# Rotary halves swapped by VectorE out of PSUM, routing cut to what the first expert needs, and the last experts' pieces in another order

## Chip, cores and metric

One core of one Trainium2 chip runs the whole program as one launch. The metric is device time in microseconds (us) of that core, the median of the runs.

## What is computed

Two blocks follow each other on 512 tokens of width 1024, in float32. The first (two layers of latent attention with a convolution, cross attention and SwiGLU) is not touched. The second is:

```python
def apply_rotary(t, cos, sin):                 # q and k of attention (24 heads) and of retention (8 heads)
    t1, t2 = jnp.split(t.astype(jnp.float32), 2, axis=-1)        # halves of 32 channels
    return jnp.concatenate([t1 * c - t2 * s, t1 * s + t2 * c], axis=-1)

def hierarchical_moe(x2, ...):                 # 8 groups of 8 experts, 2 experts of one group per token
    group_p = softmax(x2 @ w_group + b_group);  g_w, g_idx = top_k(group_p, 1)
    sel_logits = (x2 @ w_expert + b_expert) of the chosen group
    e_w, e_idx = top_k(softmax(sel_logits), 2); e_w = e_w / sum(e_w)
    gate = g_w * e_w;  eid = g_idx * 8 + e_idx
    ... # each token's row goes to its two experts: (silu(xb @ w1[e]) * (xb @ w3[e])) @ w2[e]
    ... # y[token] = sum of gate * its two rows
```

Between them stand dilated window attention, retention in both directions and a gated merge. After the experts comes a residual sum and an RMS norm.

## The kernel before

**Lanes and marks.** Five programs (TensorE, ScalarE, VectorE, GpSimd as POOL, SyncE) are written in order by hand. Every instruction may tick a semaphore and note a mark (`e.tick("both")`), and others wait for the mark (`e.wait_ge(*at("both"))`). PSUM's eight banks go round in one queue: `banks.take` takes the bank given back longest ago and waits for the mark that `banks.give` named.

**Weight pieces.** `pieces` lists all weights as pieces of up to 1 MB (`self.plan`) in the order of use. SyncE issues one load after the other, each into the slot of `self.slots` with the same number. TensorE appends a slot again when it has used a piece (`release`), so piece n waits until the slot's last piece was used. Until the merge there are three slots; a piece is split there into a high and a low part (ScalarE copies the high part, VectorE subtracts, lines 558 and 566) and a product takes three matmuls per 128 channels. The experts' weights are not split: six pieces per expert (w1, w3 and w2, two each), in thirteen slots: the three, two early ones, five late ones, two in `xT` and one in `norm_room`.

**Attention.** Four pairs of heads. A pair has 14 items (`pair_items`): six products of q and k, [128 channels, 512 tokens] each, and eight of v. The first pair's items run back to back; those of the next pair are laid two by two into the 8 steps of a pair. A step is: scores `near` and `far`, an item, transposes of the probabilities of two steps before, an item, the output of three steps before. A q or k item is rotated in this way: ScalarE copies the bank to `raws`, TensorE multiplies `swap_a` (a permutation with signs) with it (`rotate_pe`), VectorE multiplies the swapped bank with the sine table, POOL the raw copy with the cosine table, and VectorE adds them (`rotate_dve`, `rotate_pool`). The swap of item n - 1 stands behind the product of item n.

**Retention.** After the gate (four pieces) come four products for q and four for k (`retention_pe`, line 1982), each followed directly by its swap. VectorE and ScalarE also make the decay tables there.

**Router.** `router_pe` (line 2307) transposes the normalised tokens of tiles 2 and 3 and multiplies four tiles with the router's weights. `router_dve` (line 2400) chooses the group and two experts by one-hot rows, exponentiates through ScalarE, makes the gates, `picks` (one-hot rows of 64 experts for each choice) and `both`. TensorE counts with triangular and all-one matrices (14 products of 64 columns: rank of every token in its expert, and the totals). Then VectorE makes `local` (rank in the expert or -1), the table of further blocks (used only where an expert has over 64 tokens), and the slots of both choices for the final combine.

**Experts.** `experts_pe` (line 2566) runs n = 0 to 65. For even n it gathers the rows of experts n and n + 1 by multiplying the one-hot matrix `chosen` with the tokens, and turns them; for n from 1 on: the products w1 and w3 of expert n - 1, then the w2 product of expert n - 2, then the transposes of expert n - 1's hidden rows. `chosen` is made by VectorE from `local` (`experts_dve`, line 2652). ScalarE applies silu, copies and stores. In the combine, POOL fetches each token's two rows from DRAM and VectorE adds them up.

Of the kernel before, what the change touches and what calls it, by code (L numbers as in the profile page):

```python
# [16 lines left out]
P = 128  # L17
# [37 lines left out]
NEG = -1.0e30  # L55
VCOLS = NG * P // 2
# [134 lines left out]
class Net:  # L191
# [69 lines left out]
    def memory(self):  # L261
# [7 lines left out]
        self.swap_a = self.sb("swap_a", [P, P])  # L269
# [158 lines left out]
        self.local = carve("local", NT, EXPERTS)  # L428
# [34 lines left out]
    def pieces(self):  # L463
# [53 lines left out]
        for half in range(2):  # L517
            by_rows("mixer out", a["w_out_2"][0], 0, KD, half * BANK, (half + 1) * BANK)
        for ex in range(EXPERTS):
            for name in ("moe_w1_2", "moe_w3_2", "moe_w2_2"):  # L520
# [283 lines left out]
    def setup_act(self, e):  # L804
# [9 lines left out]
        for name, dst, src in (("pos", self.pos_i, a["positions"][0].partition_broadcast(P)),  # L814
                               ("freq", self.freq, a["c_freq"]), ("cols", self.cols[:, :], a["cols"]),
                               ("swap_q", self.swap_q[:, :], a["c_swap_q"]), ("mask_q", self.mask_q, a["c_mask_q"]),
                               ("swap_a", self.swap_a[:, :], a["c_swap_a"])):
            e.dma_start(dst, src).then_inc(*e.lands("setup_loads", "setup_landed", name))
# [19 lines left out]
    def angles_dve(self, e):  # L838
# [7 lines left out]
        e.wait_ge(*self.at("setup_landed", "swap_a"))  # L846
# [890 lines left out]
    def rotate_pe(self, e, pair, n):  # L1737
        bank = self.banks.take(e, "a_swap", pair, n)
        e.wait_ge(*self.at("a_raw", pair, n))
        e.matmul(bank[:, :], self.swap_a[:, :], self.raws[(pair * 2 * NG + n) % 2], start=True, stop=True).then_inc(  # L1740
            *e.tick("pe", "a_swap", pair, n))
        self.banks.give(("a_swap", pair, n), "a_sin", pair, n)
# [10 lines left out]
    def rotate_pool(self, e, pair, n):  # L1753
        raw = self.raws[(pair * 2 * NG + n) % 2]
        e.wait_ge(*self.at("pe", "a_swap", pair, n))
# [4 lines left out]
    def item_pe(self, e, pair, item):  # L1760
        kind, n = item
        if kind == "qk":
# [11 lines left out]
            if n:  # L1774
                self.rotate_pe(e, pair, n - 1)
# [11 lines left out]
        if n == 0:  # L1787
            self.rotate_pe(e, pair, 2 * NG - 1)
# [193 lines left out]
    def retention_pe(self, e):  # L1982
# [3 lines left out]
        for label in ("retention q", "retention k"):  # L1986
            for c4 in range(4):
# [6 lines left out]
                if c4 % 2:  # L1994
                    self.release(e, n)
                banks.give((label, c4), "r_raw", label, c4)
                bank = banks.take(e, "r_swap", label, c4)
                e.wait_ge(*at("r_raw", label, c4))
                e.matmul(bank[:, :], self.swap_a[:, :], self.raw_r[c4 % 2], start=True, stop=True).then_inc(
                    *e.tick("pe", "r_swap", label, c4))  # L2000
                banks.give(("r_swap", label, c4), "r_sin", label, c4)
# [101 lines left out]
    def retention_dve(self, e):  # L2103
# [38 lines left out]
        for label, buf in (("retention q", self.q_r), ("retention k", self.k_r)):  # L2142
            for c4 in range(4):
                if c4 % 2 == 0:
                    self.dve_piece(e, label)
                e.wait_ge(*at("pe", "r_swap", label, c4))
                e.tensor_tensor(buf[:, c4, :], self.bank("r_swap", label, c4)[:, :], self.sin_r, ALU.mult).then_inc(
                    *e.tick("r_sin", label, c4))
# [43 lines left out]
    def retention_pool(self, e):  # L2192
# [9 lines left out]
        for label in ("retention q", "retention k"):  # L2202
            for c4 in range(4):
                raw = self.raw_r[c4 % 2]
                e.wait_ge(*self.at("pe", "r_swap", label, c4))
# [101 lines left out]
    def router_pe(self, e):  # L2307
# [7 lines left out]
        for i in range(NT):  # L2315
            if i < 2:
                self.rows_to_T_pe_f32(e, i + 2)
# [685 lines left out]
```

## Time and profile before

| | |
|---|---|
| median of 3 runs | 3482.52 us (3480.45 to 3487.75) |
| the profiled execution | 3485.61 us, its span 3483.7 us |
| TensorE busy | 3244.1 us, 93% |
| VectorE busy | 1316.7 us, 38% |
| ScalarE busy | 876.0 us, 25% |
| POOL busy | 131.3 us, 4% |
| mean granted clock of TensorE | 0.961 |
| attention | about 1596 to 1960 us |
| retention | about 1960 to 2198 us |
| merge | 2198 to 2403 us |
| router up to the first gather | 2403 to 2453 us |
| experts | 2453 to 3444 us, DMA at 425 to 426 GB/s from 2530 on |
| combine | 3444 to 3484 us |

PE is TensorE's matmuls, PEld its weight loads, DVE VectorE, ACT ScalarE. A name ending in q (SPq) is an engine's queue at which DMAs are issued. An f32 product is recorded as two matmul instructions. "[2.54 <-DMA piece]" behind a row is the idle time of the engine before it and what ended it. L120 and the like are lines of small wrappers, so rows are told apart by the names of their tiles.

### The profile page before, as it was taken

The numbers are of one execution on the slowest core, as the hardware profiler recorded it, in microseconds if no ns is written. First come the engines' busy times: TensorE is split into PE (matmuls) and PEld (weight loads), VectorE is DVE, ScalarE is ACT, GpSimd is POOL, SyncE is SP. The second block draws the span as 40 slices with busy tenths as digits, with TensorE's granted clock in tenths as the row PEclk, the third lists the DMA queues.
The fourth block names the chain that finished last, engine by engine and source line by source line (L and its number), as shares of the span: only waits on it lengthen the run. The fifth ranks groups of instructions, "written<-read, shape, count | busy, mean of one in ns | idle before, by whom it ended". The sixth has DMA issues, their size and how long they took to land.

```text
span 3483.7 us, 35772 instructions
## 1 busy us (share of the span) xinstructions
PE 3244.1 (93%) x15128; PEld 2240.5 (64%) x15128; DVE 1316.7 (38%) x2223; ACT 876.0 (25%) x1387; POOL 131.3 (4%) x122
## 2 busy tenths in 40 slices
PE   9999999999999999998999989998799999999994
PEld 7677788887677788886888766677333433334341
DVE  5765633345765633334334436434211111111112
ACT  3452322222442222222333421222111111111111
POOL 0000000000000000001001010001000000000001
PEclk9999999999999999999999999998899999999997
DMA  4122123223122122232213220225699999999996
GB/s 170 59 85 85 61 91 103 94 100 112 60 85 85 61 91 97 97 109 80 67 45 98 66 73 31 67 97 192 250 426 426 426 425 426 426 425 426 426 425 239
DMA packets 229541, 627.62 MB, mean 180 GB/s; under 512 B 14784, under 2 KB 136512, under 8 KB 179968
## 3 DMA queue, kind: packets, MB, share of 16 engines
q1 hardware_dynamic: 207888, 581.47, 43.1%
q10 hardware_dynamic: 19296, 35.68, 2.9%
q0 software_dynamic: 2192, 8.13, 0.8%
q8 instruction: 121, 1.98, 0.2%
q14 instruction: 44, 0.36, 0.0%
HBM read 600.32 MB, written 22.81 MB: 179 GB/s over the span
## 4 chain that ended last, share of the span: by engine, by line
PE 67%; DMA 17%; DVE 10%; ACT 2%; POOL 2%; issue 1%; ACTq 0%; SPq 0%; DVEq 0%; POOLq 0%
PE bank L120 65%; DMA piece<-in_moe_w 4%; DMA piece_high<-in_moe_w 3%; DMA mT_slot<-in_moe_w 3%; DMA xT<-in_moe_w 3%; DVE gate_acc L138 2%; PE bank L123 2%; DVE x_tok L138 1%; POOL root L135 1%; DMA memT<-in_moe_w 1%; DMA norm_room<-in_moe_w 1%; DMA y_att_slot<-in_moe_w 1%; DVE stat L153 1%; DVE piece_rounded L135 1%; ACT piece_high_rounded L126 1%
## 5 line engine op out<-in xcount | busy, mean ns | idle before, releaser
L120 PE MATMUL bank<-xT_rounded,piece_high_rounded 128*128 128x512 f32 (+1 forms) x1408 | 550.5, 391 | 6.2 <-DVE xT_low_rounded L135 6.2
L135 DVE TENSOR_TENSOR piece_rounded<-piece,piece_high_rounded 128x2048 fp32r<-128x2048 f32 (+1 forms) x156 | 342.4, 2198 | 558.9 <-ACT piece_high_rounded L126 558.7
L120 PE MATMUL bank<-xT_rounded,piece_rounded 128*128 128x512 f32 (+1 forms) x1408 | 538.3, 382 | 0.0
L120 PE MATMUL bank<-xT_low_rounded,piece_high_rounded 128*128 128x512 f32 (+1 forms) x1408 | 534.3, 379 | 0.0
L135 DVE TENSOR_TENSOR gate_and_hidden<-gate_and_hidden,bank 64x512 f32<-64x512 f32 x64 | 69.2, 1081 | 836.9 <-ACT gate_and_hidden L126 836.9
L126 ACT ACTIVATE piece_high_rounded<-piece 128x2048 fp32r<-128x2048 f32 (+1 forms) x156 | 283.4, 1820 | 261.7 <-DMA piece<-in_ffn_w_down 102.3
L120 PEld LDWEIGHTS bank<-xT_rounded,piece_high_rounded 128*128 128x128 f32 x1408 | 266.2, 189 | 61.9 <-DVE xT_low_rounded L135 7.4
L120 PEld LDWEIGHTS bank<-xT_low_rounded,piece_high_rounded 128*128 128x128 f32 x1408 | 265.8, 189 | 55.9 <-issue 4.4
L120 PEld LDWEIGHTS bank<-xT_rounded,piece_rounded 128*128 128x128 f32 x1408 | 264.4, 188 | 56.4
L120 PE MATMUL bank<-piece,xeT 128*64 128x512 f32 x488 | 239.4, 645 | 18.7 <-DMA norm_room<-in_moe_w 6.1
L120 PE MATMUL bank<-piece_high,xeT 128*64 128x512 f32 x464 | 185.3, 630 | 12.3 <-DMA piece<-in_moe_w 9.0
L120 PE MATMUL bank<-xT,xeT 128*64 128x512 f32 x312 | 161.3, 666 | 14.7 <-DMA piece_high<-in_moe_w 9.1
L126 ACT ACTIVATE gate_and_hidden<-bank 64x512 f32<-64x512 f32 x64 | 37.9, 592 | 499.7 <-PE bank L120 499.7
L138 DVE SCALAR_TENSOR_TENSOR gate_acc<-hT,cols,gate_acc 128x512 f32<-128x512 f32 x240 | 163.2, 743 | 0.0
L120 PE MATMUL bank<-mT_slot,xeT 128*64 128x512 f32 x304 | 151.7, 655 | 11.7 <-DMA piece_high<-in_moe_w 11.7
L120 PE MATMUL bank<-piece_high_rounded,xT_rounded 128*128 128x192 f32 (+1 forms) x448 | 150.3, 336 | 4.4 <-DVE xT_low_rounded L135 2.7
L120 PE MATMUL bank<-piece_high_rounded,xT_low_rounded 128*128 128x192 f32 (+1 forms) x448 | 147.2, 329 | 0.0
L120 PE MATMUL bank<-piece_rounded,xT_rounded 128*128 128x192 f32 (+1 forms) x448 | 146.7, 327 | 0.0
L120 PE MATMUL bank<-piece_high_rounded,hidT_rounded 128*128 128x512 f32 x352 | 138.1, 392 | 0.0
L120 PE MATMUL bank<-piece_rounded,hidT_rounded 128*128 128x512 f32 x352 | 137.5, 391 | 0.0
L120 PE MATMUL bank<-piece_high_rounded,hidT_low_rounded 128*128 128x512 f32 x352 | 137.5, 391 | 0.0
L120 PEld LDWEIGHTS bank<-piece,xeT 128*64 128x64 f32 x488 | 69.4, 147 | 88.5 <-issue 88.5
(337 smaller groups left out, 5050.8 us busy)
## 6 DMA issues: line engine op xcount, KB each, us to landing
piece<-in_moe_w SPq DMA_DIRECT2D x90, 1024.0 KB, 16.5
piece_high<-in_moe_w SPq DMA_DIRECT2D x88, 1024.0 KB, 16.5
xT<-in_moe_w SPq DMA_DIRECT2D x59, 1024.0 KB, 16.6
mT_slot<-in_moe_w SPq DMA_DIRECT2D x58, 1024.0 KB, 17.1
piece<-in_ffn_w_in SPq DMA_DIRECT2D x40, 1024.0 KB, 5.1
memT<-in_moe_w SPq DMA_DIRECT2D x30, 1024.0 KB, 15.8
y_att_slot<-in_moe_w SPq DMA_DIRECT2D x30, 1024.0 KB, 16.7
norm_room<-in_moe_w SPq DMA_DIRECT2D x29, 1024.0 KB, 16.9
```

The costliest lines, as they stand in the source:

```text
L120: return self.engine.matmul(*a, **k) if self.engine is not None else Nothing()
L123: return self.engine.transpose(*a, **k) if self.engine is not None else Nothing()
L126: return self.engine.activation(*a, **k) if self.engine is not None else Nothing()
L135: return self.engine.tensor_tensor(*a, **k) if self.engine is not None else Nothing()
L138: return self.engine.scalar_tensor_tensor(*a, **k) if self.engine is not None else Nothing()
L153: return self.engine.bn_stats(*a, **k) if self.engine is not None else Nothing()
```

## The change

1. Swaps. `swap_a`, its load, `rotate_pe` and the swap products of retention go. VectorE multiplies each group of 32 lanes of the product's own bank with the sine table and writes it to the neighbouring group of lanes; the signs are in the table. The bank is given back only after that (before: after ScalarE's copy). POOL's cosine product waits for ScalarE's copy. For k of retention the scale is applied in the four operations.
2. Router. Tile 3's transposes move behind tile 1's products. Products by one-hot rows of the four tiles are joined into single operations; `both` is made from the sum of the one-hot rows; rank is four wide products and the totals get a bank and products of their own. `local` is FAR * both - rank in one operation, compared with FAR - iota. The counts and the table of further blocks (`counts_dve`), slots (`slots_dve`) and gates (`gates_dve`, `gates_act`) move into the first turns of the experts' loops.
3. Last experts. The plan's last pieces are w1, w3 of expert 62, w1, w3 of 63, then w2 of both; at n = 64 the transposes of expert 63's hidden rows stand before the w2 product of expert 62.

```diff
+        for ex in range(EXPERTS):
+            for name in ("moe_w1_2", "moe_w3_2"):
+                for part in range(2):
+                    self.up_pieces.setdefault(ex, []).append(len(plan))
+                    plan.append((name, self.together(a[name][0, ex], part), False))
+            for ready in () if ex == EXPERTS - 2 else (ex,) if ex < EXPERTS - 2 else (ex - 1, ex):
+                for part in range(2):
+                    self.down_pieces.setdefault(ready, []).append(len(plan))
+                    plan.append(("moe_w2_2", self.together(a["moe_w2_2"][0, ready], part), False))
...
-    def rotate_pe(self, e, pair, n):
-        bank = self.banks.take(e, "a_swap", pair, n)
-        e.matmul(bank[:, :], self.swap_a[:, :], self.raws[(pair * 2 * NG + n) % 2], start=True, stop=True).then_inc(
+    def swapped(self, b):
+        other = b + 1 - b % 2 * 2
+        return slice(b * 32, (b + 1) * 32), slice(other * 32, (other + 1) * 32)
...
     def rotate_dve(self, e, pair, n):
-        e.wait_ge(*self.at("pe", "a_swap", pair, n))
-        e.tensor_tensor(buf, self.bank("a_swap", pair, n)[:, :], self.sin_a, ALU.mult).then_inc(*e.tick("a_sin", pair, n))
+        e.wait_ge(*self.at("pe", "a_qk", pair, n))
+        e.wait_ge(*self.at("a_raw", pair, n))
+        for b in range(4):
+            to, other = self.swapped(b)
+            e.tensor_tensor(buf[to, :], bank[other, :], self.sin_a[other, :], ALU.mult).then_inc(
+                *(e.tick("a_sin", pair, n) if b == 3 else e.tick()))
...
-            self.banks.give(("a_qk", pair, n), "a_raw", pair, n)
+            self.banks.give(("a_qk", pair, n), "a_sin", pair, n)
...
-                e.matmul(bank[:, :], self.swap_a[:, :], self.raw_r[c4 % 2], start=True, stop=True).then_inc(
+                for b in range(4):
+                    to, other = self.swapped(b)
+                    e.scalar_tensor_tensor(out=buf[to, c4, :], in0=self.bank(label, c4)[other, :],
+                                           scalar=RQK ** -0.5 if label == "retention k" else 1.0,
+                                           in1=self.sin_r[other, :], op0=ALU.mult, op1=ALU.mult).then_inc(
...
-            if i < 2:
-                self.rows_to_T_pe_f32(e, i + 2)
+            if i % 2 == 0:
+                self.rows_to_T_pe_f32(e, 2 + i // 2)
...
-        for i in range(NT + 1):
-            last = min(i, NT - 1)
-            for j in range(last + 1):
-                ins = e.matmul(bank[:, i * EXPERTS:(i + 1) * EXPERTS], self.tri if j == i else self.ones,
+        e.matmul(bank[:, 0:NT * EXPERTS], self.tri, both, start=True, stop=False).then_inc(*e.tick())
+        for n in range(1, NT):
+            ins = e.matmul(bank[:, n * EXPERTS:NT * EXPERTS], self.ones, both[:, 0:(NT - n) * EXPERTS], start=False,
+                           stop=(n == NT - 1))
+        bank = banks.take(e, "count")
+        for j in range(NT):
+            ins = e.matmul(bank[:, 0:EXPERTS], self.ones, self.both[:, j, :], start=(j == 0),
...
+        e.tensor_tensor(self.t8, ohs[0], ohs[1], ALU.add).then_inc(*e.tick())
+        e.tensor_tensor(self.both.rearrange("p i (g e) -> p i g e", g=GROUPS),
+                        oh_g.unsqueeze(3).broadcast_to([P, NT, GROUPS, PER_GROUP]),
+                        self.t8.unsqueeze(2).broadcast_to([P, NT, GROUPS, PER_GROUP]), ALU.mult).then_inc(*e.tick("both"))
+        e.wait_ge(*at("pe", "rank"))
+        e.scalar_tensor_tensor(out=self.local.rearrange("p i e -> p (i e)"), in0=self.both.rearrange("p i e -> p (i e)"),
+                               scalar=FAR, in1=self.bank("rank")[:, 0:NT * EXPERTS], op0=ALU.mult,
+                               op1=ALU.subtract).then_inc(*e.tick("local"))
...
     def experts_pe(self, e):
+            if n == EXPERTS:
+                self.hidden_T_pe(e, n - 1)
             if n < EXPERTS and n % 2 == 0:
                 self.rows_T_pe(e, n // 2)
...
-            if 1 <= n <= EXPERTS:
+            if 1 <= n < EXPERTS:
                 self.hidden_T_pe(e, n - 1)
...
     def experts_act(self, e):
+            if n == 1:
+                self.gates_act(e)
...
     def experts_dve(self, e):
             if n < EXPERTS and n % 2 == 0:
                 self.rows_T_dve(e, n // 2)
+            if n == 0:
+                self.counts_dve(e)
+            if n in (1, 2):
+                self.slots_dve(e, n - 1)
+            if n == 3:
+                self.gates_dve(e)
```

## Rows read from the trace of the kernel before

**Rows 1.** The page, part 4: the chain of waits by engine, shares of the span.
```profile
PE 67%; DMA 17%; DVE 10%; ACT 2%; POOL 2%; issue 1%; ACTq 0%; SPq 0%; DVEq 0%; POOLq 0%
```
**Rows 2.** Windows: start:end, length, busy us per engine, granted clock, DMA share, GB/s.
```profile
2440.00:2450.00 10.00, 0.00 (x0) 0.00 (x0) 9.11 (x27) 0.00 (x0) 0.00 (x0) 0.50 0.00 0
...
2510.00:2520.00 10.00, 9.29 (x48) 3.68 (x48) 2.37 (x3) 1.03 (x3) 0.00 (x0) 1.00 1.02 429
```
**Rows 3.** Timeline of TensorE, first pair: start, duration, engine, line, tiles.
```profile
1615.22 1.02 PE L120 MATMUL bank<-raws,swap_a 128*128 128x512 f32 x2
...
1621.58 1.02 PE L120 MATMUL bank<-raws,swap_a 128*128 128x512 f32 x2
```
**Rows 4.** The chain in order of time, attention and retention: start, duration, what.
```profile
1750.12 15.85 PE bank L120 x70
1766.62 15.85 PE bank L120 x70
...
1970.34 33.88 PE bank L120 x144
...
2023.32 6.64 PE bank L120 x26
2030.63 6.64 PE bank L120 x26
...
2070.24 55.40 PE bank L120 x244
```
**Rows 5.** Groups of VectorE by form: count, busy us, mean ns, idle before.
```profile
L135 DVE TENSOR_TENSOR piece_rounded<-piece,piece_high_rounded 128x2048 fp32r<-128x2048 f32 x39 | 89.0, 2289 | 138.7 <-ACT piece_high_rounded L126 138.7
...
L135 DVE TENSOR_TENSOR gate_and_hidden<-gate_and_hidden,bank 64x512 f32<-64x512 f32 x64 | 69.2, 1081 | 836.9 <-ACT gate_and_hidden L126 836.9
...
L135 DVE TENSOR_TENSOR heads_q<-turn_raw,turn_sin 32x512 f32<-32x512 f32 x16 | 10.9, 684 | 3.0 <-POOL turn_raw L135 2.6
```
**Rows 6.** Timeline of VectorE in retention.
```profile
2133.74 2.47 DVE L135 TENSOR_TENSOR weigh<-bank,memT 128x512 f32<-128x512 f32 x4
```
**Rows 7.** Timeline of VectorE in the router.
```profile
2420.86 0.46 DVE L135 TENSOR_TENSOR logits<-bank,router_b 128x288 f32<-128x288 f32 x1 [12.21 <-PE bank L120]
...
2422.47 0.19 DVE L135 TENSOR_TENSOR g<-logits,v 128x32 f32<-128x32 f32 x1
...
2430.82 0.42 DVE L135 TENSOR_TENSOR both<-picks,picks 128x256 f32<-128x256 f32 x1
2437.57 0.42 DVE L129 COPY rank<-bank 128x256 f32<-128x256 f32 x1 [6.33 <-PE bank L120]
...
2438.82 0.23 DVE L132 TENSOR_SCALAR extra<-bank 128x64 f32<-128x64 f32 x1
...
2444.19 0.42 DVE L135 TENSOR_TENSOR wide<-picks,rank 128x256 f32<-128x256 f32 x1
...
2451.93 0.89 DVE L135 TENSOR_TENSOR chosen_rounded<-iota,local 128x128 fp32r<-128x128 f32 x4
```
**Rows 8.** Timeline of TensorE, router's products and first gather.
```profile
2408.71 1.97 PE L123 MATMUL bank<-ident,hn_low 128*128 128x128 f32 x8 [2.25 <-DVE hn_low L138]
2410.47 10.36 PE L120 MATMUL bank<-router_w,xT 128*128 128x72 f32 x48
...
2452.87 0.79 PE L120 MATMUL bank<-hn_high_rounded,chosen_rounded 128*128 128x512 f32 x1 [15.34 <-DVE chosen_rounded L135]
```
**Rows 9.** Timeline of SyncE's DMA queue: first issue after each release.
```profile
2467.66 0.33 SPq L162 DMA_DIRECT2D piece<-in_moe_w  x1
...
2482.66 0.33 SPq L162 DMA_DIRECT2D mT_slot<-in_moe_w  x1
```
**Rows 10.** Timeline of TensorE, last expert.
```profile
3425.83 1.09 PE L120 MATMUL bank<-piece,xeT 128*64 128x512 f32 x1 [2.54 <-DMA piece<-in_moe_w]
...
3434.25 1.90 PE L120 MATMUL bank<-memT,ehidT 128*64 128x512 f32 x8
...
3440.32 1.94 PE L120 MATMUL bank<-piece_high,ehidT 128*64 128x512 f32 x8 [2.07 <-ACT ehidT L126]
```

More of the change, by code:

```diff
@@ L2447, in router_dve @@
-        for n in range(2):
-            for i in range(NT):
-                out = picks[n][:, i, :].rearrange("p (g e) -> p g e", g=GROUPS)
-                e.wait_ge(*e.own())
-                e.tensor_tensor(out, oh_g[:, i, :].unsqueeze(2).broadcast_to([P, GROUPS, PER_GROUP]),
-                                ohs[n][:, i, :].unsqueeze(1).broadcast_to([P, GROUPS, PER_GROUP]), ALU.mult).then_inc(
-                    *e.tick())
-        e.wait_ge(*e.own())
-        e.tensor_tensor(self.both, picks[0], picks[1], ALU.add).then_inc(*e.tick("both"))
@@ L2457, in router_dve @@
-        bank = self.bank("rank")
-        rank, local = self.rank, self.local
-        e.wait_ge(*at("pe", "rank"))
-        e.tensor_copy(rank.rearrange("p i e -> p (i e)"), bank[:, 0:NT * EXPERTS]).then_inc(*e.tick())
-        count = bank[:, NT * EXPERTS:(NT + 1) * EXPERTS]
-        e.wait_ge(*e.own())
-        e.scalar_tensor_tensor(out=local, in0=rank, scalar=1.0, in1=self.both, op0=ALU.add, op1=ALU.mult).then_inc(*e.tick())
-        e.wait_ge(*e.own())
-        e.tensor_scalar(local, local, -1.0, None, ALU.add).then_inc(*e.tick("local"))
@@ new lines, in counts_dve @@
+    def counts_dve(self, e):
+        at = self.at
+        rank, ends, extra = self.rank, self.ends, self.extra
+        gmax, m1, m2, d_ = self.v4[0], self.v4[3], self.v4[4], self.v4[5]
+        e.tensor_tensor(self.g8, self.logits[:, :, 0:GROUPS], gmax.unsqueeze(2).broadcast_to([P, NT, 8]),
+                        ALU.subtract).then_inc(*e.tick("g8"))
+        e.tensor_tensor(d_, m2, m1, ALU.subtract).then_inc(*e.tick("apart"))
+        e.tensor_copy(rank.rearrange("p i e -> p (i e)"), self.bank("rank")[:, 0:NT * EXPERTS]).then_inc(
+            *e.tick("rank_copied"))
+        count = self.bank("count")[:, 0:EXPERTS]
+        e.wait_ge(*at("pe", "count"))
@@ L2487, in router_dve, with gates_dve @@
         e.tensor_copy(self.more_i, self.more_f).then_inc(*e.tick("more"))
[L2488 to L2493 removed]
+    def gates_dve(self, e):
+        at = self.at
+        gsum, d_, r_ = self.v4[1], self.v4[5], self.v4[6]
+        e.wait_ge(*at("g8_exp"))
+        e.tensor_reduce(gsum, self.g8, AX.X, ALU.add).then_inc(*e.tick())
+        e.wait_ge(*e.own())
+        e.reciprocal(gsum, gsum).then_inc(*e.tick())
+        e.wait_ge(*at("apart_exp"))
+        e.tensor_scalar(r_, d_, 1.0, None, ALU.add).then_inc(*e.tick())
+        e.wait_ge(*e.own())
+        e.reciprocal(r_, r_).then_inc(*e.tick())
+        e.wait_ge(*e.own())
+        e.tensor_tensor(self.moe_gates[0], gsum, r_, ALU.mult).then_inc(*e.tick())
+        e.wait_ge(*e.own())
+        e.tensor_tensor(self.moe_gates[1], self.moe_gates[0], d_, ALU.mult).then_inc(*e.tick())
@@ new lines, in slots_dve @@
+    def slots_dve(self, e, n):
+        rk, ex, bg, fl = self.v4[7:11]
+        pick, wide = self.picks[n], self.wide
+        e.wait_ge(*e.own())
+        e.tensor_tensor(pick.rearrange("p i (g e) -> p i g e", g=GROUPS),
+                        self.oh_g.unsqueeze(3).broadcast_to([P, NT, GROUPS, PER_GROUP]),
+                        self.ohs[n].unsqueeze(2).broadcast_to([P, NT, GROUPS, PER_GROUP]), ALU.mult).then_inc(*e.tick())
+        for out, by in ((rk, self.rank), (ex, self.row(self.iota64, EXPERTS)), (bg, self.row(self.begins, EXPERTS))):
@@ L2511, in gather_pe @@
+        e.scalar_tensor_tensor(out=self.slot_f[n], in0=bg, scalar=float(CAP), in1=rk, op0=ALU.mult,
+                               op1=ALU.add).then_inc(*e.tick())
+        e.wait_ge(*e.own())
+        e.tensor_copy(self.slot_i[n], self.slot_f[n]).then_inc(*e.tick("slots", n))
     def gather_pe(self, e, q):
```

147 lines of the change are left out of this document (59 added, 88 removed).

## The prediction

> **What bounds the kernel now.** I read the chain of waits first. By engine it is 67% TensorE, 17% DMA and 10% VectorE [rows 1], so a microsecond taken off TensorE counts wherever the chain runs on it. Then the windows. In 2440:2450 TensorE does nothing, VectorE is 91% busy and the DMA moves 0 GB/s; in 2510:2520 it moves 429 GB/s at a share of 1.02 [rows 2]. From about 2483 to 3425 the kernel is one saturated stream of expert weights (384 pieces of 1 MB, one in 2.46 us at 427 GB/s). The stream has 13 slots; they fill before the first expert is computed, and then the DMA stands until TensorE gives slots back. TensorE's granted clock in 2440:2450 is 0.50, the lower of its two levels (1.2 GHz), with TensorE idle [rows 2]; "half clock" below means that. So the end follows the moment at which the stream runs for good. Three places can move it: attention and retention (TensorE-bound, ahead of it), the routing (ahead of the first released slots), and what comes after the last piece.
>
> **Attention's swaps, 24 products.** A rotation now costs one f32 product of 512 columns. Swap follows swap after 6.36 us in the first pair [rows 3]; between them lie 24 products at 0.229 us, 5.50 us. So a swap takes 0.86 us of TensorE. Nothing hid it: TensorE has no gap there, and a step with two such items starts 16.50 us after the one before [rows 4]. Removed: 24 x 0.86 = 20.6 us.
>
> What is added lies on VectorE: one 128x512 multiplication becomes four of 32x512. The trace of before has no 32-lane operation that reads PSUM in another group of lanes than it writes, four in a row. Nearest rows: a 32x512 product whose inputs and output lie in different groups of 32 lanes took 684 ns; the dearest 512-element product, with strided operands and one in PSUM, 1081 ns [rows 5]; four 128x512 products out of PSUM back to back took 2.47 us together, 0.62 each [rows 6]. Bounds of one: 0.62 and 1.08 us. I take 0.72, the first row plus the 0.03 us seen between waiting neighbours, since it has the same lanes and size. Four make 2.9 us in place of 0.69, so 2.2 us more per rotation.
>
> Is there room? A heavy step (two rotations) shrinks to 16.50 - 1.72 = 14.8 us. VectorE does in it: softmax 2.1, one split of a weight piece 2.3 [rows 5], two rotations of 2.9 + 0.7, together 11.6 us. The rotation of the first item follows the split, which waits for ScalarE's half of it; laid out in order, VectorE is done some 0.8 us before the next scores are. Even late scores don't stop TensorE, which transposes them two steps later. The bank of a product is now held until VectorE has read it, about 11 us into the next step; banks go round seven at a time and six are taken per step, so it is wanted 4 us after that. In the first pair an item costs VectorE 2.9 + 0.7 + 1.15 (half a split) = 4.8 us against TensorE's 5.5. The cover holds; cost zero. Without it each 0.1 us of a multiplication would cost 0.8 us in each of 9 heavy steps.
>
> A rule of the Trainium skill speaks against the four: VectorE: DVE Perf Modes, section "Two Vector instructions with no wait between them", says that an instruction whose inputs or output start in another quadrant than those of the one before is held until everything earlier has finished. By it the four don't overlap, 4 x 0.72; without it they would run like rows 6, 2.5 us. No row shows four such in a row; the sum moves by about 1 us, in retention.
>
> **Retention's swaps, 8 products.** Here TensorE also waits each time for ScalarE's copy. A period is 7.31 us, of which 5.50 is the product [rows 4]. The whole, from the gate's end at 2004.2 to the end of the last swap at 2071.1, takes 66.9 us, the wait behind the decay tables included (chain rows at 1970.34 and 2070.24). After: 8 x 5.50 = 44.0, if splits come in time. VectorE needs per item 2.9 + 0.7 + 1.15, and 2.4 once for tables: 40 us for eight, so it follows closely; laid out in order, the split of the second piece of k comes about 1.8 us late (behind the rotations of q and the table that ScalarE needs first). I take 46 us. Gain 21 us; bounds 14 (0.86 + 0.85 each and no more, 8 times) and 23.
>
> **Routing, up to the first gather.** Before, the last router product ends at 2420.83 and the gather starts at 2452.87 [rows 8].
> - The fourth tile's transposes now come after the second tile's products, so the 2.25 us idle before 2408.71 is filled by 16 products [rows 8]. If these run at the full clock they vanish there: 16 x 0.216 = 3.4 us gained. At half clock from the start 2.2; if filling the gap keeps the clock up for all, 7. I take 3.4.
> - The vector chain up to both took 10.38 us (2420.86 to 2431.24 [rows 7]). Counted anew: logits 0.49; three choices of the best, 15 small operations of 0.22; two small ones more; the masked logits, their sum and the final product at 0.45 each: 5.6 us. Gain 4.8.
> - Rank: 28 instructions, 6.3 us, to 2437.57 [rows 7]. Now products of 256, 192, 128 and 64 columns. At half clock a 512-column product costs 1.72 (twice the 0.86), a short one not under 0.43: 0.86 + 0.64 + 0.43 + 0.43 = 2.4 us. Gain 3.9.
> - From rank to gather 15.3 us [rows 7, 8]: two copies, counts, the further blocks' table, both slot chains. Now one operation out of PSUM (0.45) and the comparison (0.93), beside 8 count instructions on TensorE, 1.75 us, which stand in front of the gather: 1.8 us. Gain 13.5.
> Together 25.6 us: the gather starts near 2427.3 by the old clock. POOL's low halves (done 2421.6) and the first pieces (landed by then) don't hold it.
>
> What was moved comes back. The counts (6.2 us) run after the xeT copies while TensorE is in expert 0's 7.1 us product: they end 1.6 us ahead of need. The slots of choice 0 (0.45 + 3.9 us from 2444.19, [rows 7]) now stand before the comparison for experts 2 and 3; TensorE's next gather and expert 1's product are queued behind it: 4.4 us later, and 0.5 us more for a longer time at half clock. The rest (second slots, gates, ScalarE's two exponentials and two table loads) falls into gaps of 8 to 13 us. The first four slots were released at 2467.66, the next four at 2482.66 [rows 9]; four pieces are 9.8 us, so the DMA stood again before 2482.66. It runs for good from that second release, which moves by 25.6 - 4.9 = 20.7 us. Bounds 9 and 25.
>
> **The tail.** Expert 63's first weights now come two pieces earlier in the stream, 4.9 us. Its product started at 3425.83 after 2.54 us of waiting for the DMA, ran 3 us at half clock and ended at 3434.25 [rows 10]. Now it starts at 3423.4, in an unbroken run, and needs 6.9 to 7.0 us: 3430.4. Then silu, product and transposes (2.4 us), and both outputs, 3.6 us each: 3440.0 in place of 3443.98 (from 3440.32 plus 3.66). Gain 4.0 us, bounds 1 and 5. The two last down pieces land by 3430.3. The combine behind it doesn't change.
>
> Sum: 20.6 + 21 + 20.7 + 4.0 = 66.3 us. The profiled execution took 3485.6 us (span 3483.7 and 1.9 around it): 3419.3 by its own time. The median of the runs lies 3.1 us lower, which gives 3416 us.
>
> **Rivals.**
> - Postponed routing costs its full length. All 16.4 us of counts, slots and gates delay the first slots; for it: they stand in VectorE's queue before work that TensorE needs. Against: VectorE idles 8 us (2460.4 to 2468.3) there. Then the routing yields 25.6 - 16.4 = 9 us, the time is 3428. Chance 0.15.
> - VectorE becomes the bound of rotations. At 1.08 us per multiplication the heavy step still fits (14.5 of 14.8); the first pair's items take 6.2 instead of 5.5, retention's 6.5 instead of 5.75: 10 us lost, 3426. For it: 1081 ns in rows 5. Against: those operands are strided. Chance 0.1.
> - The clock stays up over the router's products and rank, and the second gather is hardly late: 6 to 9 us more, 3408. Chance 0.12.
> - Slower: shifted reads out of PSUM go lane group by lane group and cost D. A heavy step is then 5.8 + 8D, a first item 1.85 + 4D, a retention item 2.15 + 4D, against 16.5, 6.36 and 8.4 before. With 24.7 us gained elsewhere the sum is zero at D = 1.54 us; at 2.2 us it is 128 x 0.66 = 84 us slower, 3567. Only the 684 ns row, not out of PSUM, speaks against it. Chance 0.03.
> - The change doesn't do what it says, for example since banks held longer stop TensorE as much as the swaps did: 3455 to 3480. Chance 0.02.
>
> **How the numbers follow.** My forecast has 0.58: 3416, own range 3409 to 3424. With the first three rivals and the bounds of the terms the range for 8 in 10 is 3402 to 3434. A measurement of this kernel tells about 0.2%, 7 us. Faster 0.96, within 0.01, slower 0.03.
>
> **What would show it.** No swap products; TensorE still without gaps in 1600 to 1900 and heavy steps near 14.8 us; 32x512 products near 0.69 us; retention's q and k in about 46 us; the first gather 10 us after the last router product instead of 32; the first two releases of slots about 19.9 us apart instead of 15.0; experts' DMA share unchanged; last product's end to combine unchanged. It is wrong if TensorE waits for VectorE in attention, if the second release comes over 25 us after the first, or if the stream has gaps later.

## The result, and the profile after

The changed kernel takes 3441.97 us (median of 4 runs, 3437.72 to 3446.06), the kernel before 3484.17 us beside it: a ratio of 0.9879, 95% interval 0.9861 to 0.9897. It is 42 us faster. 3416 us was forecast, with a range of 3402 to 3434 us; the time lies 8 us above that range.

The profiled execution has a span of 3444.2 us instead of 3483.7. Page, part 1 (busy us by engine) and part 4 (the chain by engine, which answers to [rows 1]):

```profile
PE 3215.6 (93%) x15052; PEld 2226.0 (65%) x15052; DVE 1387.9 (40%) x2311; ACT 876.3 (25%) x1388; POOL 136.7 (4%) x122
...
PE 65%; DMA 17%; DVE 12%; ACT 3%; POOL 2%; issue 1%; ACTq 0%; SPq 0%; DVEq 0%; POOLq 0%
```

VectorE's share of the chain grew from 10 to 12%: some of its work stands on the path now. By stages, cut at the same instructions in both traces (us saved, of 39.5):

| stage | before | after | saved | forecast |
|---|---|---|---|---|
| start to first attention product | 1596.40 | 1598.96 | -2.6 | 0 |
| attention | 373.9 | 375.0 | -1.0 | 20.6 |
| retention's q, k and v (end of the gate's products to the last v product) | 111.7 | 93.6 | 18.1 | 21 |
| retention's gate, rest of retention, merge | 321.6 | 320.8 | 0.8 | 0 |
| third tile's transposes to first released slots | 64.0 | 40.5 | 23.5 | 25.6 |
| first to second release | 15.0 | 20.5 | -5.5 | -4.9 |
| second release to the end | 1001.0 | 994.9 | 6.1 | 4.0 |

Attention is where the forecast failed. Its heavy steps (two q/k items) are as forecast, 14.8 us from softmax to softmax in the second and third pair. The first light steps (two v items) behind them are not. VectorE's timeline, second pair (start, duration, engine, line, operation, tiles; each `aprobs<-bank,masks` is one step's softmax):

```profile
1787.21 0.69 DVE L142 CUSTOM_DVE_ANT_0 aprobs<-bank,masks 128x512 f32<-128x512 f32 x1 [1.81 <-PE bank L121]
...
1791.11 1.76 DVE L136 TENSOR_TENSOR piece_rounded<-piece,piece_high_rounded 128x1536 fp32r<-128x1536 f32 x1 [1.75 <-ACT piece_high_rounded L127]
1792.90 2.84 DVE L136 TENSOR_TENSOR ks<-bank,sin_a 32x512 f32<-32x512 f32 x4
1795.84 0.69 DVE L136 TENSOR_TENSOR ks<-ks,raws 128x512 f32<-128x512 f32 x1
1801.14 0.69 DVE L142 CUSTOM_DVE_ANT_0 aprobs<-bank,masks 128x512 f32<-128x512 f32 x1 [4.61 <-PE bank L121]
```

The next softmaxes come at 1801.14, 1812.82 and 1821.95: steps of 13.93 and 11.68 us, then 9.13. Before, the same two took 10.00 and 9.12. TensorE's timeline at that place, its waits in attention (us in total, times, longest), and the windows (columns as in [rows 2]):

```profile
1793.08 0.28 PE L121 MATMUL bank<-piece_high_rounded,xT_low_rounded 128*128 128x192 f32 x1
1795.79 0.43 PE L121 MATMUL bank<-aprobsT,vs 128*64 128x128 f32 x2 [2.44 <-DVE ks L136]
```
```profile
PE bank L121 <- DVE ks L136: 6.9, 3, 2.4
```
```profile
1786.00:1798.00 12.00, 9.56 (x72) 8.73 (x70) 7.24 (x13) 4.02 (x8) 0.52 (x1) 0.93 0.22 79
1798.00:1806.00 8.00, 8.00 (x31) 6.55 (x30) 2.04 (x7) 1.03 (x2) 0.00 (x0) 0.50 0.01 2
1806.00:1840.00 34.00, 34.00 (x242) 29.51 (x242) 11.29 (x30) 12.85 (x24) 0.00 (x0) 0.99 0.19 63
```

Read together: the last q/k product's bank comes free when VectorE has multiplied out of it. VectorE first splits the piece of v, and that split waits until 1791.11 for ScalarE's half. Only then come the four multiplications, whose last ends at 1795.74. TensorE wanted the bank at 1793.35 and stands for 2.44 us. Behind the wait its granted clock is 0.50 (1.2 GHz) for the whole window from 1798 to 1806, with TensorE busy throughout. Such a wait comes once in three of the four pairs: 2.0 us in the first, 2.44 us in each of the next two.

The router. TensorE's products now stand between the transposes (the third tile's begin at 2388.32), all at the full clock:

```profile
2389.20 3.69 PE L121 MATMUL bank<-router_w,xT 128*128 128x72 f32 x32
2393.37 1.09 PE L124 MATMUL bank<-ident,hn_low 128*128 128x128 f32 x8 [0.48 <-DVE hn_low L139]
2394.29 3.69 PE L121 MATMUL bank<-router_w,xT 128*128 128x72 f32 x32
```

The last ends 9.7 us after the third tile's transposes begin. Before, these began at 2403.68 and the last product ended 17.2 us later, at 2420.83 [rows 8]. VectorE's chain behind it, and GpSimd beside it:

```profile
2398.74 2.14 DVE L136 TENSOR_TENSOR t<-logits,v 128x32 f32<-128x32 f32 x1
2400.91 2.26 DVE L136 TENSOR_TENSOR t<-t,down 128x32 f32<-128x32 f32 x1
2403.21 0.19 DVE L148 TENSOR_REDUCE v<-t 128x4 f32<-128x32 f32 x1
2403.43 2.04 DVE L136 TENSOR_TENSOR oh_g<-down,v 128x32 f32<-128x32 f32 x1
...
2407.05 0.19 DVE L136 TENSOR_TENSOR t<-t,down 128x32 f32<-128x32 f32 x1
...
2409.29 0.42 DVE L136 TENSOR_TENSOR both<-oh_g,t 128x256 f32<-128x256 f32 x1
```
```profile
2396.16 9.26 POOL L136 TENSOR_TENSOR hn_low_rounded<-hn_low,hn_high_rounded 128x1024 fp32r<-128x1024 f32 x4 [4.96 <-ACT hn_high_rounded L127]
```

The chain was counted at 5.6 us and takes 11.7 (from 2398.02). One and the same 128x32 operation takes 2.26 us while GpSimd works and 0.19 us after it has stopped; three such operations are stretched.

The releases (SyncE's queue, answering to [rows 9]), and what holds the second, on TensorE and VectorE:

```profile
2428.78 0.33 SPq L163 DMA_DIRECT2D piece<-in_moe_w  x1
...
2449.30 0.33 SPq L163 DMA_DIRECT2D mT_slot<-in_moe_w  x1
```
```profile
2430.49 0.42 DVE L136 TENSOR_TENSOR picks<-oh_g,ohs 128x256 f32<-128x256 f32 x1
...
2434.75 0.89 DVE L136 TENSOR_TENSOR chosen_rounded<-from_far,local 128x128 fp32r<-128x128 f32 x4
```
```profile
2435.70 0.80 PE L121 MATMUL bank<-hn_high_rounded,chosen_rounded 128*128 128x512 f32 x1 [4.73 <-DVE chosen_rounded L136]
```

The slots of choice 0 run from 2430.49 to 2434.84 and the comparison for experts 2 and 3 stands behind them, as forecast. The last two experts, by the chain in order of time, answer to [rows 10]:

```profile
3389.54 7.04 PE bank L121 x32
...
3398.78 7.04 PE bank L121 x32
```

### The profile page after: what moved, and what is told of

Its sections match the earlier page's. It is cut to its first block, busy times and chain, and to the rows that moved or that the text cites. A ratio compares the mean times of both kernels' runs of the same rounds, so it can differ in the third digit from the quotient of the medians.

```text
span 3444.2 us, 35709 instructions
## 1 busy us (share of the span) xinstructions
PE 3215.6 (93%) x15052; PEld 2226.0 (65%) x15052; DVE 1387.9 (40%) x2311; ACT 876.3 (25%) x1388; POOL 136.7 (4%) x122
## 4 chain that ended last, share of the span: by engine, by line
PE 65%; DMA 17%; DVE 12%; ACT 3%; POOL 2%; issue 1%; ACTq 0%; SPq 0%; DVEq 0%; POOLq 0%
PE bank L121 63%; DMA piece_high<-in_moe_w 4%; DMA mT_slot<-in_moe_w 3%; DMA piece<-in_moe_w 3%; DMA xT<-in_moe_w 3%; DVE gate_acc L139 2%; PE bank L124 2%; DVE x_tok L139 2%; POOL root L136 1%; DMA memT<-in_moe_w 1%; DVE piece_rounded L136 1%; DMA norm_room<-in_moe_w 1%; DMA y_att_slot<-in_moe_w 1%; ACT piece_high_rounded L127 1%; DVE stat L154 1%
## 5 line engine op out<-in xcount | busy, mean ns | idle before, releaser
L121 PE MATMUL bank<-piece_high,xeT 128*64 128x512 f32 x464 | 187.1, 642 | 15.4 <-DMA piece<-in_moe_w 9.3
```

Source lines behind the costliest of these rows:

```text
L121: return self.engine.matmul(*a, **k) if self.engine is not None else Nothing()
```

## Experiments

All are the changed kernel with one edit. "Release" is the first DMA issue after the first or second set of slots came free, counted from the third tile's transposes.

**1. The sine products ahead of the split.**

```diff
     # item_dve, v items
-        if n % NT == 0:
-            self.dve_piece(e, "attention v")
         if n == 0:
             self.rotate_dve(e, pair, 2 * NG - 1)
+        if n % NT == 0:
+            self.dve_piece(e, "attention v")
```

> The changed kernel, with VectorE making the sine products of the last q/k item ahead of its split of the v piece, so that the bank of the last q/k product comes free about 1.8 us earlier. Theory A (attention's gain went into a bank that TensorE waits for, and into the half clock that follows): the 2.4 us wait of the 12 attention products on bank and aprobsT in pairs 2 and 3 goes to under 0.8 us, the granted clock stays at 1.00 in the 10 us behind it, the two steps of 13.9 and 11.7 us of each pair come to 9.2 to 10 us each, and the kernel takes 15 to 20 us less than the changed one (3422 to 3427 us). Rival A2 (VectorE's added work is what binds attention, whatever its order): the steps lengthen as before, the wait only moves, and the time stays within 2 us of the changed kernel's 3442 us. Rival A3 (the wait goes but the v piece's split is late by 2.8 us and TensorE waits for that instead): the wait of the v product of 2 to 3 us takes its place, gain 0 to 5 us.

Measured: 3423.39 us, ratio 0.9828 (0.9812 to 0.9845), 18.6 us below the changed kernel. VectorE:

```profile
1778.74 2.84 DVE L136 TENSOR_TENSOR ks<-bank,sin_a 32x512 f32<-32x512 f32 x4
1781.69 0.69 DVE L136 TENSOR_TENSOR ks<-ks,raws 128x512 f32<-128x512 f32 x1
1782.30 1.75 DVE L136 TENSOR_TENSOR piece_rounded<-piece,piece_high_rounded 128x1536 fp32r<-128x1536 f32 x1
1785.70 0.69 DVE L142 CUSTOM_DVE_ANT_0 aprobs<-bank,masks 128x512 f32<-128x512 f32 x1 [1.65 <-PE bank L121]
```

TensorE's waits in attention have no entry for `ks` any more. From softmax to softmax, the light steps behind the heavy ones of the second and third pair are 9.12 or 9.13 us and the heavy ones 14.8; attention takes 353.8 us, 20.1 less than before the change, where 20.6 was forecast. The same instructions fit, so VectorE's added work doesn't bind attention (A2 falls). TensorE's one wait for a split there is 1.2 us, against 1.0 in the changed kernel, so the split is not late (A3 falls).

**2. Attention's products back.** Retention, routing and tail stay as changed.

```diff
+        bank = self.banks.take(e, "a_swap", pair, n)
+        e.wait_ge(*self.at("a_raw", pair, n))
+        e.matmul(bank[:, :], self.swap_a[:, :], self.raws[(pair * 2 * NG + n) % 2], start=True, stop=True).then_inc(
+            *e.tick("pe", "a_swap", pair, n))
...
-        for b in range(4):
-            to, other = self.swapped(b)
-            e.tensor_tensor(buf[to, :], bank[other, :], self.sin_a[other, :], ALU.mult).then_inc(
+        e.tensor_tensor(buf, self.bank("a_swap", pair, n)[:, :], self.sin_a, ALU.mult).then_inc(*e.tick("a_sin", pair, n))
```

> The changed kernel, with attention's halves swapped by TensorE's 24 products as in the kernel before, and the rest (retention, routing, order of the last pieces) as changed. Theory A: attention's part of the change gave only 1.1 us in the profiled execution, so this one takes 0 to 3 us more than the changed kernel (3442 to 3445 us), with heavy steps of 16.5 us, no step of 13.9 us and no half clock in them. Rival (the swaps' removal is worth its 20.6 us, and what is lost was lost elsewhere, as in the first 1600 us): 15 to 20 us more, about 3460 us.

Measured: 3441.06 us, 0.9881 (0.9864 to 0.9897), the same as the changed kernel. Attention takes 374.7 us, with steps of 16.5, 10.0 and 9.12. So the measured gain of 42 us came from the other three parts, within the 8 us or so that the two ratios leave open.

**3. The wait doubled.**

```diff
+        for b in range(4 if n == 2 * NG - 1 else 0):
+            to, other = self.swapped(b)
+            e.tensor_tensor(buf[to, :], bank[other, :], self.sin_a[other, :], ALU.mult).then_inc(*e.tick())
+        if n == 2 * NG - 1:
+            e.wait_ge(*e.own())
```

> The changed kernel, with VectorE's four sine multiplications of the last q/k item of each pair made twice (the second time with the same values), so that the bank of that product comes free about 2.9 us later. Theory A (the bank wait, and the clock behind it, are what attention lost): TensorE's three longest waits grow from 2.4 to about 5.3 us, so pairs 2, 3 and 4 lose 2.9 us each or more, 8.7 to 14 us in all, and the kernel takes 3450 to 3458 us. Rival (the wait shown is only where the time is booked, and VectorE had room there): the waits and the time stay within 2 us of the changed kernel's.

Measured: 3454.35 us, 0.9922 (0.9906 to 0.9939), 13.5 us above the changed kernel run beside it (4). TensorE's waits:

```profile
PE bank L121 <- DVE ks L136: 15.5, 3, 5.3
```

```profile
1802.00:1815.00 13.00, 12.24 (x54) 10.65 (x55) 3.42 (x9) 1.97 (x5) 0.00 (x0) 0.54 0.00 1
```

The waits grow by 2.9 us each, by what is added to VectorE in front of the bank, 8.6 us in all; the step with the wait goes from 13.9 to 17.2 us. The window lies behind the second pair's wait. Attention takes 385.9 us, 10.9 more than in the first trace, where the half clock also stood behind all three waits, and 22.8 more than in the trace of (4), where it stood behind one only. So the waits account for 8.6 us; that the rest is a longer time at half clock fits the windows, but no run separates it.

**4. The changed kernel again.**

> The changed kernel once more, without an edit. Four profiles with its attention code have had attention lengths of 375.0, 369.8, 372.4 and 366.4 us, and the start of attention between 1594.2 and 1599.2 us, though no instruction there differed. If the half clock behind the bank wait is a matter of how long TensorE is held at it, and not of the instructions, this run lies among them: attention 366 to 376 us, start 1594 to 1600 us, median 3436 to 3446 us. Rival (the differences came from the edits after all): 375.0 us and 1599.0 us within 0.5 us.

Measured: 3440.9 us, runs from 3427.65 to 3442.87, 0.9885 (0.9868 to 0.9901). The profiled one has a span of 3425.9 us, attention of 363.1 us (below the 366 expected) and a start at 1593.64 us. The waits are the same, the clock behind them is not; the second pair's wait lies in this window:

```profile
PE bank L121 <- DVE ks L136: 6.9, 3, 2.4
```
```profile
1782.00:1790.00 8.00, 5.56 (x42) 4.61 (x41) 5.42 (x9) 0.61 (x3) 0.00 (x0) 1.00 0.01 2
```

Here the clock stays at 1.00 and the steps are 11.64 and 9.12 us: the bare wait costs 2.5 us. With the half clock behind it, as in the trace after, it costs 7.4 (13.93 + 11.68 against 2 x 9.12). Seven profiles with this same attention code and this wait gave 375.0, 363.1, 372.4, 369.8, 366.4, 375.9 and 373.4 us, the two without the wait 353.8 and 353.9. The -2.6 us ahead of attention belongs to such scatter too: the start lies between 1593.6 and 1599.6 us in the twelve profiles, and the changed kernel alone had it at 1593.6 and at 1599.0.

**5. The low halves on VectorE.** They are made while it waits for the router's products.

```diff
     # router_dve, behind from_far; removed from router_pool
+        for i in range(NT):
+            e.wait_ge(*at("hn_high", i))
+            e.wait_ge(*at("pe", "hnT", i, 4))
+            self.low_of(e, self.hn_low[:, i, :], self.hn_low[:, i, :], self.hn_high[:, i, :]).then_inc(*e.tick("hn_split", i))
     # router_act: each high half straight behind its tile, not all four at the end
+                self.high_of(e, self.hn_high[:, i - 1, :], self.hn_low[:, i - 1, :]).then_inc(*e.tick("hn_high", i - 1))
```

> The changed kernel, with the low halves of the four normalised tiles made by VectorE before it waits for the router products, in place of GpSimd, and ScalarE's high halves one at a time behind its evictions. Theory B (VectorE's operations with two inputs in SBUF are held up while GpSimd's tensor_tensor runs): the three small 128x32 operations take 0.2 us each again in place of 2.1, the chain from the last router product to the last condition takes 5.6 to 6.2 us in place of 11.7, and the kernel takes 4 to 6 us less (3436 to 3438 us). Rival B2 (the small operations are slow for what they read, whatever GpSimd does): they stay near 2.1 us and the time stays or grows by what VectorE's four low halves take (about 4 us). Rival B3 (the chain is short but the four low halves start too late on VectorE and push it back): chain 5.6 us, start 3 to 5 us later, gain 0 to 2 us.

Measured: 3434.20 us, 0.9862 (0.9845 to 0.9879). VectorE:

```profile
2386.90 4.61 DVE L136 TENSOR_TENSOR hn_low_rounded<-hn_low,hn_high_rounded 128x1024 fp32r<-128x1024 f32 x4
2391.58 0.46 DVE L136 TENSOR_TENSOR logits<-bank,router_b 128x288 f32<-128x288 f32 x1
...
2392.30 0.19 DVE L136 TENSOR_TENSOR t<-logits,v 128x32 f32<-128x32 f32 x1
...
2396.98 0.43 DVE L136 TENSOR_TENSOR both<-oh_g,t 128x256 f32<-128x256 f32 x1
```

The chain takes 5.8 us, and the comparison comes 5.9 us earlier. The first release moves from 40.5 us (38.8 in six others of these profiles, where the gather itself ran at the full clock) to 35.4, though the gather ran at a clock of 0.51 here. The four halves fit into the gap (1.15 us each instead of GpSimd's 2.3), so B3 falls. The total alone would not show it: the ratios differ by 0.0017, and their two half-widths together are 0.0025.

**6. GpSimd made to wait.** Nothing is added on VectorE.

```diff
     # router_pool, ahead of the low halves
+        e.wait_ge(*self.at("both"))
```

> The changed kernel with one wait more on GpSimd: it begins the low halves of the four tiles only when VectorE's chain of conditions has ended. No instruction is added on VectorE. Theory B (it is GpSimd's simultaneous tensor_tensor that stretches VectorE's small operations): the three 128x32 operations of 2.0 to 2.3 us take 0.19 us, the chain from the last router product to the last condition takes 5.6 to 6 us in place of 11.7; GpSimd's 9.3 us then lie behind it, where the rank, the local and the chosen operations meet them, so that the gather starts 0 to 6 us earlier than in the changed kernel or up to 4 us later: 3437 to 3446 us. Rival B2 (the operations are slow because of where they read): they stay at 2.0 to 2.3 us.

Measured: 3438.16 us, 0.9863 (0.9848 to 0.9879), runs from 3430.9 to 3448.98. GpSimd, then VectorE:

```profile
2404.66 9.35 POOL L136 TENSOR_TENSOR hn_low_rounded<-hn_low,hn_high_rounded 128x1024 fp32r<-128x1024 f32 x4 [12.73 <-DVE both L136]
```
```profile
2399.46 0.19 DVE L136 TENSOR_TENSOR t<-logits,v 128x32 f32<-128x32 f32 x1
...
2404.15 0.43 DVE L136 TENSOR_TENSOR both<-oh_g,t 128x256 f32<-128x256 f32 x1
...
2407.28 0.42 DVE L139 SCALAR_TENSOR_TENSOR local<-both,bank 128x256 f32<-128x256 f32 x1 [2.70 <-PE bank L121]
2407.73 6.62 DVE L136 TENSOR_TENSOR chosen_rounded<-from_far,local 128x128 fp32r<-128x128 f32 x4
```

The chain takes 5.8 us again, and now the comparison is stretched, 6.62 us for four instead of 0.90. The stretch goes with GpSimd's time and hits whatever VectorE does in it with two inputs in SBUF. `local`, with one input in SBUF and one in PSUM, takes its 0.42 us in the middle of it. B2 falls. The first release stays at 40.2 us: moving the place where the two engines meet gains nothing.

**7. Slots and gates behind the comparisons.**

```diff
     # experts_dve
-            if n in (1, 2):
-                self.slots_dve(e, n - 1)
-            if n == 3:
+            if n in (2, 4):
+                self.slots_dve(e, n // 2 - 1)
+            if n == 6:
```

> The changed kernel, with VectorE's two slot steps and its gates put behind the chosen pieces (n 2, 4 and 6 instead of 1, 2 and 3). Theory C (the second release is late because the first slots stand ahead of the second chosen piece on VectorE): the first two SP releases stand 15 to 16.5 us apart instead of 20.5, TensorE's 4.7 us wait for the rounded second chosen piece goes to about 0.5 us, and the kernel takes 4 to 5 us less (3437 to 3438 us). Rival (a transfer that the slots feed, or the piece's own landing, ends the second stretch): the wait at TensorE goes but the releases stay 19 to 20.5 us apart, and the time stays at 3442 us.

Measured: 3432.11 us (3423.54 to 3439.56), 0.9848 (0.9823 to 0.9873). The releases:

```profile
2421.49 0.33 SPq L163 DMA_DIRECT2D piece<-in_moe_w  x1
...
2436.74 0.33 SPq L163 DMA_DIRECT2D mT_slot<-in_moe_w  x1
```

They are 15.25 us apart, not 20.5 (19.4 to 19.6 in six others of these profiles): the delay was the slots, as forecast, and it is worth 4 to 5 us. The median fell further than that, by 10 us, but its runs are 16 us apart, and attention, not edited, took 5.2 us less in this profile than in the first.

**8. Retention's products back.**

```diff
-                banks.give((label, c4), "r_sin", label, c4)
+                banks.give((label, c4), "r_raw", label, c4)
+                bank = banks.take(e, "r_swap", label, c4)
+                e.wait_ge(*at("r_raw", label, c4))
+                e.matmul(bank[:, :], self.swap_a[:, :], self.raw_r[c4 % 2], start=True, stop=True).then_inc(
+                    *e.tick("pe", "r_swap", label, c4))
+                banks.give(("r_swap", label, c4), "r_sin", label, c4)
```

> The changed kernel with retention's halves swapped by 8 products of TensorE as in the kernel before. The stretch from the end of the retention gate to the end of the v products was 121.4 us before and 103.3 us after: it goes back to about 121 us, and the kernel takes 17 to 19 us more (3459 to 3461 us). Rival (part of the 18 us came with other states of the buffers left by attention, not from the products): 112 to 118 us in the stretch and 9 to 15 us more.

Measured: 3452.14 us, 0.9915 (0.9900 to 0.9930), only 10 us above the changed kernel (the ratios differ by 0.0036, their two half-widths together are 0.0023: 4 to 21 us). In the trace the stretch, cut as in the table, grows from 93.6 to 109.0 us, by 15.4; on the expectation's scale that is 118.7, between the two theories. The windows over it, before and in this run:

```profile
2004.00:2116.00 112.00, 102.16 (x401) 76.86 (x399) 36.35 (x36) 28.11 (x28) 10.31 (x8) 0.95 0.21 71
```
```profile
2001.00:2112.00 111.00, 101.15 (x405) 76.08 (x405) 36.47 (x37) 28.73 (x29) 10.79 (x8) 0.98 0.21 72
```

The same instructions and the same eight waits, with a mean clock of 0.98 in place of 0.95. A mean of 0.95 is a tenth of the stretch at half clock, 11 us, in which 5.6 are lost; 0.98 loses 2.2. That difference of 3.4 covers the missing 2.7. The changed kernel's stretch also had a mean clock of 0.98 (2007.6 to 2101.3), so at the same clock the products cost 15.4 us, and the other 2.7 of the table's 18.1 are the clock's doing. The rival's cause, buffers left in another state by attention, doesn't show: the waits are the same.

**9. The tail undone.**

```diff
-            for ready in () if ex == EXPERTS - 2 else (ex,) if ex < EXPERTS - 2 else (ex - 1, ex):
+            for ready in (ex,):
...
-            if n == EXPERTS:
-                self.hidden_T_pe(e, n - 1)
```

> The changed kernel with the order of the last experts' pieces and transposes as before. What the tail is worth: the time behind the second release goes from 994.9 us back to about 1001 us, and the kernel takes 4 to 6 us more (3446 to 3448 us). Rival: the 6.1 us that the profile shows behind the second release come from the earlier start of the pieces and not from the tail's order; then it stays within 2 us of 3442 us.

Measured: 3441.52 us (3432.29 to 3449.38), 0.9880 (0.9859 to 0.9900): no difference that the times can show. The trace shows it: second release to the end 1001.2 us, as before the change, against 993.7 to 997.5 in the ten profiles with the new tail. The tail is worth 3.7 to 7.5 us. Attention, not edited, took 366.4 us in this profile, 8.6 less than in the first, which is more than the tail's worth and hides it in the profiled time.

**10. The three corrections together** (1, 5 and 7).

> The changed kernel with all three corrections: sine products of the last q/k item ahead of the v split, low halves of the tiles on VectorE before the router products' wait, slots and gates behind the chosen pieces. The first three runs gave, against the changed kernel, 21 us in attention, 5.1 us to the first release and 5.3 us between the releases, and 0.6 to 2 us lost again behind the second release. If the terms lie behind each other they add: 3411 to 3416 us, with 353.8 us of attention, 35.4 us from the last transposes to the first release and 15.3 us between the releases. Rival: the weights' transfers take over the bound behind the second release (11 GB/s shown there only while nothing is released, but the four large pieces then want them all earlier), so that what lies behind it grows from 995 to over 1000 us: 3418 to 3422 us.

Measured: 3412.62 us (5 runs, 3408.99 to 3416.25), 0.9799 (0.9786 to 0.9813). It is the fastest of all, 29 us below the changed kernel. Attention takes 353.9 us, the first release comes at 33.9 us, and the releases:

```profile
2399.33 0.33 SPq L163 DMA_DIRECT2D piece<-in_moe_w  x1
...
2413.03 0.33 SPq L163 DMA_DIRECT2D mT_slot<-in_moe_w  x1
```

lie 13.7 us apart. Both stretches are 1.5 us shorter than expected (35.4 and 15.3); the gather, at a clock of 0.51 in experiment 5, had 0.81 here, and from the first release to the second the clock was 1.00. Behind the second lie 996.6 us, so the weights' stream didn't take over; the rival falls.

## Why the prediction was wrong

It missed by 26.8 us of saving (66.3 forecast, 39.5 in the trace): 21.6 in attention, 2.6 ahead of it, 2.9 in retention, 2.7 in the routing, less 0.8 in the merge and 2.1 in the tail, which came out better.

**The step that failed** is attention's cover: "The bank of a product is now held until VectorE has read it, about 11 us into the next step; banks go round seven at a time and six are taken per step, so it is wanted 4 us after that. ... The cover holds; cost zero." That was laid out for a step with two q/k items, 14.8 us long. The last q/k item of a pair is rotated in the step that follows, a light one with two v items, 9.1 us long. There the bank is wanted at 1793.35, 6.1 us after the step's softmax began, and VectorE has a split first that itself waits for ScalarE. The bank came 2.0 to 2.4 us late, three times, and the clock took up to twice that again. Experiment 1 takes the wait away and gets the 20.6 us back to within 0.5; experiment 3 makes it longer and pays for each added us. The forecast's own sign of being wrong, TensorE waiting for VectorE in attention, came true. The size of the removed part (0.86 per swap), the heavy step and the price of a multiplication (0.72 forecast, 2.84 / 4 = 0.71) were right.

The forecast gave such a failure 0.02, as "banks held longer stop TensorE as much as the swaps did". For attention that is what happened. Its price there, 3455 to 3480, is too high for that: the loss of attention's 20.6 us alone makes 3437. The first rival about VectorE, throughput, was the wrong question: VectorE is idle for 4.61 us right behind the late multiplications. What counted was the order in which it works, not how much.

**Retention, 18.1 instead of 21.** Its q and k take 49.1 us (2007.6 to 2056.7), not 46. There is one wait of 3.2 us for the split of a piece (1.8 forecast), and a mean clock of 0.94 from 2033 to 2063 loses another 1.8, which the forecast had at nothing. The mechanism holds, but part of the 18.1 is luck: 2.7 come from a lower clock in the trace before (0.95 against 0.98), and the products alone were worth 15.4 (experiment 8). TensorE's only wait in 2001 to 2112, and the windows:

```profile
PE bank L121 <- DVE piece_rounded L136: 3.2, 1, 3.2
```
```profile
2033.00:2063.00 30.00, 26.82 (x111) 21.44 (x110) 25.54 (x33) 8.52 (x8) 8.01 (x4) 0.94 0.26 87
```

**Routing, to the first release 23.5 instead of 25.6.** Two errors of opposite sign, so that the small miss is luck. The router's products gained 7.5, not 3.4: the clock stayed up over all of them, the case that the forecast named at 7 and put among the rivals. The chain was 11.7 us, not 5.6, since GpSimd's low halves now lie beside it; before, they ran while VectorE waited (a 12.2 us wait stands in [rows 7]). "POOL's low halves ... don't hold it" looked only at when their results were needed. Experiments 5 and 6 show the collision. From `both` to the gather it took 4.1 us instead of 21.6, a gain of 17.5 where 17.4 was forecast.

**Between the releases, 5.5 lost, 4.9 forecast.** Experiment 7 shows the cause that was named.

**Tail, 6.1 instead of 4.0.** The last product's end moved by 4.8 us against the second release, and 1.3 came behind it, where the forecast had no change; the cause of that is open. The product runs unbroken in 7.04 us, as forecast.

What stays open: which waits pull the clock down in a given run. The same wait of 2.4 us was followed by 1.2 GHz in one execution and by 2.4 GHz in another. The Trainium skill, TensorE: Matmul & The Clock Gate, section "What's actually happening", says that one kernel has a different number of slow matmuls at its start from run to run, since the chip's look at activity isn't tied to the program. The two traces agree that the slow stretches differ; they don't show the reason.

## What to carry to other kernels

When a helper engine takes over the last read of a buffer, find the shortest step in which that read falls, not the longest, and count what stands in the helper's queue before it, with that work's own waits. Put the operation that frees a TensorE buffer first in the queue. Before work is moved earlier, look at what another engine does at the new time: an idle engine's old work may only have been free because of where it lay.

## What the runs showed of the hardware

- VectorE's operations with two inputs in SBUF took 2.0 to 2.3 us instead of 0.19 us while GpSimd ran four `tensor_tensor` instructions of 2.3 us each; a reduction (one input) beside them stayed at 0.19, and an operation with one input in SBUF and one in PSUM at 0.42 (experiment 6). The Trainium skill, SBUF — State Buffer, section "SBUF: two separate sides", says that the two engines share a pair of ports, that an operation with two SBUF inputs against a GpSimd operation that reads SBUF waits until the whole instruction is done, and that they don't share by halves. The rows agree: each stretched operation took about one of GpSimd's.
- Four multiplications of 32x512, each writing another group of 32 lanes than it reads out of PSUM, take 2.84 us, 687 ns each and 0.71 from one to the next. They don't overlap, where four 128x512 in [rows 6] took 2.47 us together, and the shift has no price beyond that of the 32x512 row in [rows 5].
- One kernel, executed again with the same waits, had spans of 3444.2 and 3425.9 us: 11.9 us of the difference lie in attention, by the clock behind three waits of 2.0 to 2.4 us, and 5.3 before it. A stage of a few us is read from its own length in the trace, not from the total.
